# Host-transposed conditioning weights and host-transposed x in a two-layer hybrid encoder kernel: row sums in place of weighted adds and TensorE column sums

## What is computed

```python
def adaln(c, w, b):
    mod = (c @ w + b)[:, None, :]
    shift, scale, gate = jnp.split(mod, 3, axis=-1)
    return shift, scale, gate

for l in range(DEPTH):                                    # DEPTH = 2
    shift, scale, gate = adaln(c, w_ada_mix[l], b_ada_mix[l])
    u = x * (1.0 + scale) + shift
    y = hybrid_mixer(u, ...)      # u @ w_in, conv group and windowed attention, @ w_out
    x = layer_norm(DN_ALPHA * x + (1.0 + gate) * y, ln1_g[l], ln1_b[l])
    shift, scale, gate = adaln(c, w_ada_ffn[l], b_ada_ffn[l])
    u = x * (1.0 + scale) + shift
    y = conv_gated_mlp(u, ...)    # u @ w_up, conv, SiLU gate, @ w_down
    x = layer_norm(DN_ALPHA * x + (1.0 + gate) * y, ln2_g[l], ln2_b[l])
```

## Time and profile before

| what | value |
|---|---|
| time, median of 3 runs | 2101.79 us (2101.77 to 2103.06) |
| the profiled execution's own time | 2101.31 us |
| its span, first to last instruction | 2099.5 us |
| mean granted TensorE clock | 0.997 of 2.4 GHz |
| TensorE matmuls busy | 2064.8 us (98%) |
| VectorE busy | 1191.1 us (57%) |
| ScalarE busy | 1031.2 us (49%) |
| GpSimd busy | 1413.6 us (67%) |
| DMA moved | 250.07 MB, 119 GB/s in the mean |
| chain that ended last | TensorE 86%, GpSimd 5%, ScalarE 3%, VectorE 3% |

### The profile page before, as it was taken

How to read it: one execution, slowest core, us unless ns; L and a number is a source line. 1 busy time by engine, 2 the same in 40 slices (tenths; PEclk the granted TensorE clock), 3 DMA queues, 4 the chain that set the end, 5 groups by cost and what they waited for, 6 DMA issues and landing times.

```text
span 2099.5 us, 27374 instructions
## 1 busy us (share of the span) xinstructions
PE 2064.8 (98%) x9619; PEld 1701.8 (81%) x9619; DVE 1191.1 (57%) x1940; ACT 1031.2 (49%) x1845; POOL 1413.6 (67%) x1780
## 2 busy tenths in 40 slices
PE   7999999999999999999999999999999999999997
PEld 6877778787888878888788888888878888888887
DVE  5888888675515554777632645587651455332235
ACT  3585356555516674374643756235562465333332
POOL 4987767755778887875557885564556776545454
PEclk9999999999999999999999999999999999999999
DMA  8644544533434354553233333332323332434332
GB/s 301 157 134 148 161 127 148 162 108 103 121 111 124 107 162 145 141 159 93 76 100 106 111 111 91 101 103 73 100 76 107 88 104 84 128 99 123 94 100 78
DMA packets 421510, 250.07 MB, mean 119 GB/s; under 512 B 48149, under 2 KB 393085, under 8 KB 421373
## 3 DMA queue, kind: packets, MB, share of 16 engines
q1 hardware_dynamic: 420506, 248.03, 39.8%
q10 hardware_dynamic: 867, 0.29, 0.1%
HBM read 242.71 MB, written 4.26 MB: 118 GB/s over the span
## 4 chain that ended last, share of the span: by engine, by line
PE 86%; POOL 5%; ACT 3%; DVE 3%; issue 2%; ACTq 0%; DMA 0%; POOLq 0%; DVEq 0%
PE fg L886 27%; PE fg L888 27%; PE fg L887 27%; POOL w_lo L1932 3%; PE bank_s L984 1%; POOL ada_acc L2003 1%; ACT ada L1324 1%; PE bank_l L915 1%; PE bank_t L993 1%; PE bank_t L1006 1%; DVE bank_c L1539 0%; POOL ssum L2030 0%; POOL u_lo L2012 0%; ACT probs L1291 0%; ACT probs L1283 0%
## 5 line engine op out<-in xcount | busy, mean ns | idle before, releaser
L1932 POOL TENSOR_TENSOR w_lo<-raw,w_hi 128x256 fp32r<-128x256 f32 (+1 forms) x1425 | 1031.3, 755 | 609.8 <-ACT w_hi L1163 608.7
L886 PE MATMUL fg<-u_hi,w_hi 128*128 128x512 f32 x2112 | 834.7, 395 | 6.2 <-DVE u_lo L1519 2.6
L888 PE MATMUL fg<-u_hi,w_lo 128*128 128x512 f32 x2112 | 823.7, 390 | 0.0
L887 PE MATMUL fg<-u_lo,w_hi 128*128 128x512 f32 x2112 | 823.5, 390 | 0.0
L1163 ACT ACTIVATE w_hi<-raw 128x1024 fp32r<-128x1024 f32 (+2 forms) x387 | 375.6, 971 | 385.6 <-PE fg L888 278.4
L886 PEld LDWEIGHTS fg<-u_hi,w_hi 128*128 128x128 f32 x2112 | 397.1, 188 | 102.5 <-issue 14.5
L888 PEld LDWEIGHTS fg<-u_hi,w_lo 128*128 128x128 f32 x2112 | 397.0, 188 | 84.2
L887 PEld LDWEIGHTS fg<-u_lo,w_hi 128*128 128x128 f32 x2112 | 397.4, 188 | 80.1 <-issue 0.5
L1539 DVE SCALAR_TENSOR_TENSOR bank_c<-glu,par,bank_c 128x512 f32<-128x512 f32 x448 | 306.1, 747 | 0.1
L1886 DVE SCALAR_TENSOR_TENSOR x<-fg,mod,x 128x512 f32<-128x512 f32 (+1 forms) x168 | 121.6, 724 | 319.3 <-PE fg L888 319.0
L888 PE MATMUL fg<-h_hi,w_lo 128*128 128x512 f32 (+1 forms) x704 | 269.8, 383 | 0.0
(11 more groups left out here) (272 smaller groups left out, 1860.8 us busy)
## 6 DMA issues: line engine op xcount, KB each, us to landing
raw<-in_w_up_dram SPq DMA_DIRECT2D x176, 512.0 KB, 3.8
ada<-in_w_ada_ffn_dram SPq DMA_DIRECT2D x48, 512.0 KB, 4.4
raw<-in_w_down_dram SPq DMA_DIRECT2D x64, 384.0 KB, 3.5
raw<-in_w_in_dram SPq DMA_DIRECT2D x40, 512.0 KB, 4.0
raw<-in_w_down_dram SPq DMA_DIRECT2D x64, 320.0 KB, 3.1
ada<-in_w_ada_mix_dram SPq DMA_DIRECT2D x32, 512.0 KB, 4.2
raw<-in_w_in_dram SPq DMA_DIRECT2D x32, 256.0 KB, 3.7
raw<-in_w_out_dram SPq DMA_DIRECT2D x32, 256.0 KB, 2.9
```

The lines of the kernel that those rows point to most:

```text
L886: pe.matmul(out, hi[:, k, :], rhi, start=k == order[0], stop=False)
L887: pe.matmul(out, hi[:, k, :], rlo, start=False, stop=False)
L888: ins = pe.matmul(out, lo[:, k, :], rhi, start=False, stop=k == order[-1])
L1932: ins = pool.tensor_tensor(lo_of(n)[:, ks, :], raw[n % NRAW][:, ks, :], hi_of(n)[:, ks, :].bitcast(F32), ALU.subtract)
```

## The change

It does the following.

1. The host passes all conditioning weights transposed, so that outputs lie on the partitions and the 1024 inputs lie in a row: `ada_first` (the 2048 outputs of the first shift and scale, as 8 tiles x 2 halves of 128x1024) and `ada_t` (the rest, 80 blocks of 128x1024). c is spread over all partitions (`c_rows[128, 2, 512]`) by two products of TensorE with a row of ones, which ScalarE copies to SBUF. A block's 128 outputs are then the row sums of block times `c_rows`.
2. First sub-layer: 16 instructions of VectorE (`first_total`), each 128x1024, multiply and sum in one, k by k: shift and scale of feature tile k. ScalarE adds the biases for tile k, makes `tmp` and `u_hi`, GpSimd makes all eight `u_lo`. Slab 0 and 1 can so be fed tile by tile. `add_first`, `first_sums`, `fold("half", ...)` and all `idle_products` are gone.
3. The other 80 blocks: GpSimd multiplies by `c_rows` (two products of 128x512, step `ad`), ScalarE copies in place with its accumulator as the row sum (new step `ae`, one slab later, moved to the end of ScalarE's steps). For chunks 8 to 10 VectorE does all in one instruction. The sums on TensorE (`as`), their evacuations and VectorE's reductions are gone. SyncE's next load of such a block now waits for ScalarE's row sum (or VectorE's).
4. x comes from the host as features by tokens, so the transposes and copies of the start and the steps `xt` are gone. The first output block is stored as features by tokens straight from `x` (steps `tm` are DMAs only), and the host turns it.

The core of the diff:

```diff
-        if c in ONES_CHUNKS:
-            at(ns[-1] + 2, "as", c)
-        else:
-            put(ns[-1] + 2, "as", c)
+        for part, n in enumerate(ns):
+            if c not in DVE_CHUNKS:
+                at(n + 1, "ae", c, part)
...
-            for t in range(TB):
-                load_x(t)
-                load_first(t)
-                if t == 1:
-                    load_w(0)
-            load_w(1)
-            for i in range(TB, len(FIRST_PIECES)):
-                load_first(i)
+            for k in range(DT):
+                load_first(k)
+                if k % 2 == 0 and k < DT // 2:
+                    load_x(0, k // 2)
+                if k == 1 or k == 3:
+                    load_w(k // 2)
+                if k == 4 or k == 5:
+                    load_x(0, k - 2)
+                if k == 5:
+                    load_rows(rows2, rows3)
...
+            for half in (0, 1):
+                pe.matmul((bank_t, bank_s)[half][:], ones_1[0:1, :], c_rows[0:1, half, :], start=True, stop=True).then_inc(set_pe, 1)
...
             def first_inputs(k):
-                if k % (DT // 2) == 0:
-                    act.wait_ge(fold_step, FOLDED["half", 2 * k // DT])
...
+                act.wait_ge(first_one, 1)
+                act.wait_ge(first_sum, 2 * k + 1)
+                act.activation(bias[:, 0, k:k + 1], mod[:, 0, 0, k:k + 1], ACT.Identity,
+                               bias=par1[:, 0, OFF["b_ada_mix"] + k:OFF["b_ada_mix"] + k + 1]).then_inc(first_fold, 1)
+                act.wait_ge(first_sum, 2 * k + 2)
+                act.activation(gain[:, 0, k:k + 1], mod[:, 0, 0, DT + k:DT + k + 1], ACT.Identity, bias=scale_0[:, k:k + 1]).then_inc(first_fold, 1)
...
+                if k >= 2:
+                    act.wait_ge(ilo, k - 1)
+                inputs(tmp[:, k % 2, :], xs(0, k), 0, k, iu)
                 inputs(u_hi[0][:, k, :], xs(0, k), 0, k, ihi)
...
-            def ada_scale(c, part):
+            def ada_total(c, part):
                 m = (c - CHUNKS_BEFORE) * QUARTERS + part
...
+                act.wait_ge(ada_mul, 2 * sum(ada_engine(i) == "act" for i in range(m + 1)))
+                rows = ada[m % 2][:].rearrange("p h n -> p (h n)")
+                act.activation(rows, rows, ACT.Copy, accum_out=total_of(c, part)).then_inc(ada_done["act"], 1)
...
+            def first_total(k, half):
+                dve.wait_ge(in_first[k][half], 16)
+                rows, c = first_ada[k][:, half, :], half * DT + k
+                dve.scalar_tensor_tensor(out=rows, in0=rows, scalar=1.0, in1=c_rows[:].rearrange("p h n -> p (h n)"),
+                                         op0=ALU.mult, op1=ALU.mult, accum_out=mod[:, 0, 0, c:c + 1]).then_inc(first_sum, 1)
...
+            def ada_weigh(c, part):
                 m = (c - CHUNKS_BEFORE) * QUARTERS + part
...
+                pool.wait_ge(in_ada[m % 2], 16 * (m // 2 + 1))
+                pool.wait_ge(set_col, 2)
+                for i in (0, 1):
+                    pool.tensor_tensor(ada[m % 2][:, i, :], ada[m % 2][:, i, :], c_rows[:, i, :], ALU.mult).then_inc(ada_mul, 1)
...
-            for n in range(2):
-                split_lo(n)
-            for k in range(DT // 2):
+            split_lo(0)
+            for k in range(DT):
+                if k == 2:
+                    split_lo(1)
+                if k == 4:
+                    angles(0)
                 first_lo(k)
-            angles(0)
             split_lo(2)
...
+def first_rows(w):
+
+    return np.ascontiguousarray(w[:, :2 * D].T.reshape(2, DT, P, D).transpose(1, 0, 2, 3))
```

More of the change, by code:

```diff
@@ L380, in plan @@
     for t in range(TB):
-        put(346 + 2 * t, "tm", t)
+        at(346 + 2 * t, "tm", t)
     put(330, "rows")
@@ L484, in build @@
         ada = [sb(f"ada{i}", [P, 2, T]) for i in range(2)]
-        ada_acc = [sb(f"ada_acc{i}", [P, T]) for i in range(2)]
+        c_rows = sb("c_rows", [P, 2, T])
         tmp = sb("tmp", [P, 2, T])
@@ L838, in take @@
                 held[bank] = s, n
-            def transposes(out, half, src):
-                for k in range(4):
-                    ins = pe.transpose(out[:, k * P:(k + 1) * P], src(half * 4 + k), ident)
-                return ins
-            def x_to_features(t, banks):
-                pe.wait_ge(in_x[t % 4], 16 * (t // 4 + 1))
-                for half in (0, 1):
-                    if banks[half] is bank_t or banks[half] is bank_s:
-                        take("ts"[half], x_evac[half], t + 1)
-                    transposes(banks[half], half, lambda k: stage_in[t % 4][:, k * P:(k + 1) * P]).then_inc(x_t_done, 1)
             def u_ready(kind, l, b, k):
@@ L1394, in _ @@
                     split_hi(n + NHI)
-                for step in STEPS[n]:
+                for step in sorted(STEPS[n], key=lambda step: step[0] == "ae"):
                     what = step[0]
@@ L1419, in _ @@
                         a_hi(*step[1:])
-                    elif what == "ad" and step[1] not in DVE_CHUNKS:
-                        ada_scale(*step[1:])
-                    elif what == "xt":
-                        evac_x(step[1], (bank_t, bank_s))
-                    elif what == "as" and step[1] in ONES_CHUNKS:
-                        copy_ada(step[1])
+                    elif what == "ae":
+                        ada_total(*step[1:])
                     elif what in ("ch", "xh"):
@@ L1820, in background @@
                 elif what == "ad":
-                    add_ada(*step[1:])
-                elif what == "as" and step[1] not in ONES_CHUNKS:
-                    reduce_ada(step[1])
+                    ada_total(*step[1:])
                 elif what == "fold":
@@ L2120, in _, with ada_engine @@
             pool.tensor_tensor(stage_out[2][:, 0:T], stage_out[2][:, 0:T], b_rows[:, 0:T], ALU.add).then_inc(y_pool, 1)
[L2124 to L2128 removed]
+def ada_engine(m):
+    return "dve" if CHUNKS_BEFORE + m // QUARTERS in DVE_CHUNKS else "act"
 TAIL_SMALL, TAIL_SMALL_2 = 12, 5
```

368 lines of the change are left out of this document (92 added, 276 removed).

## The result

The changed kernel takes 2123.78 us (median of four runs, 2115.15 to 2125.64) against 2101.78 us: ratio 1.0095, 95% interval 1.0067 to 1.0123. Forecast were 2096.2 us and a range of 2087 to 2111, so the change came out slower where a gain was forecast. The four runs lie 10 us apart, where those of the kernel before lie within 1.5 us; that turned out to matter.

The account below looks back on a forecast made before the run. GpSimd's queue was taken to set the pace up to slab 11, TensorE's behind it. Slab 11 7.6 us later less 12.7 us gave -5.1 us against 2101.3: 2096.2 us, range 2087 to 2111.

Parts of the forecast that it names:

- TensorE's queue: Behind slab 11: ones products 2.4, transposes of 16 chunks 6.9 and output tiles 3.4 us leave TensorE, sum 12.7 us.
- The start: Up to the first block's last `u_lo`: ends at 52.5 us, 5.7 later than before, each row sum costing GpSimd 1.10 us.
- half-rate rival: First row sums: the accumulator doubles each to 2.3 us, last `u_lo` at 69.3, result 2113 us; chance 14%.
- weak collision: Start: row sums keep up with the DMAs, last `u_lo` at 40 to 42 us, result 2084.7 us; chance 20%.
- From there to slab 11: After the first block's last `u_lo`: GpSimd works without waits, 46.9 us from slab 4's `w_lo`; slab 11 starts 7.6 us later.
- Sum: Whole kernel: 7.6 us later at slab 11 less 12.7 us behind it, -5.1 us; other edits cost nothing under TensorE's cover.
- lock step rival: Queues of SyncE, ScalarE and GpSimd hold each other up, costing 3 to 8 us: 2099 to 2104 us; chance 16%.

Follow-up runs that it names:

- selfwait: The changed kernel, with GpSimd waiting between its two products of a block for the end of the first: 2105.70 us, ratio 1.0013.
- psum_c2: selfwait, with the 16 first row sums reading c from two PSUM banks instead of the SBUF copy: 2094.73 us, ratio 0.9955.
- same_again: The changed kernel measured once more, nothing edited: 2114.45 us, ratio 1.0061.
- after: The first measurement and profile of the changed kernel, against the kernel before: 2123.78 us, ratio 1.0095.
- gap: The changed kernel, with GpSimd waiting after its rotary product of the first q for VectorE's sine product: 2110.17 us, ratio 1.0030.
- no_wait: all3 without the added wait between GpSimd's two products of a block: 2101.37 us, ratio 0.9994.
- one_product: The changed kernel with one GpSimd product of 128x1024 a block instead of two of 128x512, no wait added: 2111.27 us, ratio 1.0047.
- one_product2: one_product measured once more, nothing edited: 2115.49 us, ratio 1.0052.
- orders: selfwait with VectorE's row sums of chunks 8 to 10 and ScalarE's last ones of chunks 16, 17, 23 moved later: 2103.24 us, ratio 1.0000.
- all3: The changed kernel with the wait between products, c in PSUM for the first row sums and the two moved steps: 2093.69 us, ratio 0.9951.
- best: all3 measured once more, nothing edited, in five runs: 2091.83 us, ratio 0.9951.
- all4: all3 with the four blocks of chunk 4 moved from GpSimd and ScalarE to VectorE: 2096.45 us, ratio 0.9967.

## Why the prediction was wrong

**The steps that held.** TensorE's queue: in selfwait nearly all of the 16 chunks' transposes gave back 0.43 to 0.48 us, and the output tiles 3.56 us (four steps of 0.89), as booked (0.43 and 3.4). The start: row sum 1.22 us (1.26), last `u_lo` at 52.63 (52.5), `w_lo` of slab 4 at 66.15 (66.1). That the last `u_lo` came out within 0.2 us is in part luck. The sum charged GpSimd 16 x 1.10 = 17.6 us for row sums from 12.6 us on. In truth GpSimd had not begun before 18.35, so that the first row sums cost it nothing but it idled 5.8 us for `w_hi` (which ScalarE made behind a copy for which it had waited 4.00 us for TensorE); eleven row sums cost 10.9 us, and two waits for ScalarE 1.1: together 17.8. The price of one row sum was near (1.0 for 1.10; its 0.57 us for the half width is in no row, 3.35 less 2.82 in the earlier trace rows is 0.53), the path was not.

By the trace the half-rate rival and the Trainium skill's Vector Engine (DVE) Microarchitecture Reference, section 7, are refuted for this form: 1024 elements with two f32 SBUF operands and an accumulator take 1.22 us, 1.2 ns each, and as long with one of the operands in PSUM (psum_c2). The weak collision is refuted too, as a description of this kernel; psum_c2 shows that its numbers (t = 41) come true once the second SBUF operand is gone.

**The step that failed, in the first place:** "From there to slab 11", 46.9 us of GpSimd without a wait. It holds where VectorE is not starved (GpSimd is done at 113.04 us in selfwait, and slab 11 is 8.4 us late there and 8.9 in same_again, for the forecast 7.6). In the first profile of the changed kernel it broke, since GpSimd's own queue waits for VectorE through q, SyncE's swap and the weights (8.65 us idle at 98.07). I had priced every collision as one instruction waiting for one, up to 1.9 us, by the earlier trace rows. The rows of before held no longer case and I took that for a bound. Its price against selfwait: 9.2 us up to slab 11 in the first profile and another 5.1 by slab 15; in other executions 6 to 9 us at one place, or none.

Of the six profiles without an added pause in all of GpSimd's products (after, same_again, gap, no_wait, one_product, one_product2) five have a VectorE instruction of 6 to 13 us, and each began while GpSimd was at a product of line 1805 (its numbers in the edited kernels differ by a few). The six profiles with the wait between the products (selfwait, psum_c2, orders, all3, best, all4) have none among some 20 such meetings each, nor has the one with the wait behind. That the wait between removes it is shown by no_wait against best and by these counts. Why a pause there matters stays open. The kernel before, whose adds had such waits, shows no long one in its profile, which fits. How chancy it is shows in one pair: the same request 1.17 us into the product took 0.15 us in same_again and 9.10 in gap. The Trainium skill's SBUF — State Buffer page, section "SBUF: two separate sides", says that whoever comes first holds the shared ports for its whole instruction; the traces agree for the other meetings, but for the 2.19 us in same_again, and here the one who came second waited for fourteen.

**The step that failed in the second place:** "Sum", where the other edits were booked at zero. From slab 11 to the last product selfwait gains 3.0 us and not 12.7. Adding up the steps of the difference, TensorE gives back some 16 us there (the 12.7 and waits of before that are gone) and loses some 13: 1.7 from slab 11 to 12, 5.1 ahead of slab 25 (the row sum in front of the reciprocal root), 2.4 around 260 us, 2.4 at the three places where ScalarE's row sum stands ahead of `h_hi`, 1.4 near the end, which was not traced. I had named their cover (TensorE's long queue) but not asked what stands behind each row sum on its own engine; slab 22 and line 1270 would have answered it.

Not all of the 13 us are waits. 4.5 to 5 are TensorE at 1.2 GHz, a term that the sum had only for the first pair of slabs, and there at nothing. The granted clock in three stretches of selfwait, and in the kernel before:

```profile
114.70:121.50 6.80, 5.35 (x17) 4.58 (x18) 4.41 (x6) 0.15 (x1) 6.80 (x8) 0.50 0.26 82
217.10:220.50 3.40, 3.40 (x10) 2.62 (x9) 2.25 (x5) 2.98 (x5) 0.00 (x0) 0.50 0.00 0
278.50:282.00 3.50, 3.50 (x10) 2.72 (x9) 3.19 (x12) 0.00 (x0) 3.50 (x6) 0.51 0.01 2
```

```profile
60.00:2080.00 2020.00, 2008.48 (x9275) 1651.85 (x9274) 1140.32 (x1852) 1002.67 (x1802) 1372.94 (x1711) 1.00 0.39 114
```

In the low stretches products of a slab start 0.43 us apart in place of 0.23. The first fell within TensorE's wait of 4.29 us for k, the second followed on its wait of 4.14 us for `wide`; ahead of the third it had waited 0.70 us and run the small sums of a layer norm. They make most of the 1.7 us behind slab 11, 1.6 of the 5.1 and 1.6 of the 2.4 around 260 us. With the row sum moved (orders) the second stretch is gone: there the wait is 1.23 us and the clock stays at 1.00.

So the sum, with the measured sizes: +8.4 for +7.6 at slab 11 and -3.0 for -12.7 behind it give selfwait's +5.4. The changed kernel's last product is later than that by 16.9 us in the first profile and 7.0 in the second. The long instructions have 14.3 and 6.1 of these, the three places of ScalarE 3.3 and 2.6. Not every loss comes in every execution: in same_again TensorE loses 0.6 us from slab 22 to 25, not 5.1. The lock step rival names the right queues, but what stopped them was one starved instruction and not the length of their work.

## What to carry to other kernels

Where VectorE instructions with two SBUF operands run beside a GpSimd queue that never pauses, take no bound on a collision from a trace in which GpSimd does pause: give the one that matters an operand in PSUM, or GpSimd a wait between its instructions, and look at the spread of the runs. Two engines that multiply and add in SBUF cost each other time even when both have some to spare; one operand moved to PSUM was worth 11 us here. A step that leaves TensorE and lands on VectorE or ScalarE needs its place checked against the next thing TensorE waits for on that engine, and a wait of TensorE can cost more than itself: behind the 4.14 us in selfwait came 1.6 us more at half the clock.

## What the runs showed of the hardware

A VectorE instruction of 128x4, 0.15 us alone, stood 9.1 us beside uninterrupted GpSimd work, and ended when GpSimd went idle. Whether it comes differs between executions of one kernel: without a wait in the products the runs of a kernel spread over 10 to 18 us, with the wait between them over 3 to 6 (2102.57 to 2107.71 over ten runs).
